# Combination weights in slot order inside the experts' inner product, the layer gate multiplied by POOL ahead of the store, and the final scaling done tile by tile

## The chip, the cores and the metric

The kernel runs on one core of one Trainium2 chip. The metric is the device time of one execution in microseconds (us). In what follows PE is TensorE, DVE is VectorE, ACT is ScalarE, POOL is GpSimd and SP is SyncE, which here only issues DMAs. L1413 means line 1413 of the kernel as the profile counts it.

## The reference, cut to what matters

One layer for 128 context tokens and 512 latent tokens (640 rows, five tiles of 128) of width 1024. The mixer (mLSTM and differential attention) is untouched. What the change touches is the mixture of experts, its gate and the final norm:

```python
h = rmsnorm(x, norm_ffn) * (1.0 + sc2) + sh2
x = x + g2 * hierarchical_moe(h, ...)      # g2 differs between context and latent tokens
y = rmsnorm(x, final_norm)
...
# hierarchical_moe: top-1 of 4 groups, then top-2 of 4 experts in it
comb = jnp.sum(one_hot(expert_idx, 16) * (top_p * p_grp)[..., None], axis=1)
for e in range(16):
    a, u = jnp.split(x @ w_gu[e], 2, axis=-1)
    y = y + comb[:, e:e + 1] * ((silu(a) * u) @ w_dn[e])
```

## The kernel before, in words

Every engine runs a program of its own, written out by hand; the order of the work on an engine is the order of the text, and engines wait for each other on semaphores.

**Output projection and routing.** For each of the five tiles PE computes the projection in two halves (`oproj`, L1599), DVE adds the gated residual (`residual`, L1210 and L1211), ACT makes the norm, DVE writes the modulated rows h2 (`modulate`, L1225 and L1227), SP stores them to a scratch tensor in DRAM, PE transposes them (L1634) and computes 20 router logits (L1645). DVE turns these into one-hot picks (`route`, L1138 to L1162), PE ranks the picks within each expert (L1652), DVE builds a placement matrix (`place_rank`, L1169 to L1171) and PE multiplies it with the token numbers (`slot_ids`, L1662), so that slot s of expert e holds a token number (`place_id`, `idall`). `place_slot` (L1190 to L1201) computes for each token where its two results will lie, and the two weights of its two picks. DVE works through these in the order of the loop `for t in range(NT)`: rank of t-2, residual, id and slot of t-2, route of t-1, second residual, modulate of t. SP's queue in the same stage holds, in this order: the four broadcast loads of scale and shift (`mod2`), the two of the layer gate g2 (`g2b`), the final norm's vector, the weights of the first two experts, the stores of h2.

**The experts.** A round gives each expert 128 slots; the routing decides at run time how many rounds there are (`n_rounds`), and this input takes one. Within a round the 16 experts go through in 8 pairs (b = 0, 1). POOL gathers 128 rows of h2 for each expert of a pair (L602, an indirect DMA) one pair ahead; PE transposes them into the PSUM banks 2b and 2b+1 (L1706); DVE copies them out (L1269); PE multiplies by the gate and up weights (L1713); ACT makes silu (L824); DVE multiplies it with u (L1274); PE transposes that (L1720, L1734); DVE copies (L1277); PE multiplies by the down weights into the same banks 2b and 2b+1 (L1728); ACT copies the result to SBUF (L828, L829) and stores it to a second scratch tensor (L831). The transposes of the next pair wait until ACT has emptied the banks (`yo_ready`). SP streams the weights.

**After the experts.** POOL gathers for each token tile the rows of its two picks (ten indirect DMAs, L612). ACT scales the first by its weight (L840), DVE multiplies the second by its weight and adds (L1308), multiplies by g2 (L1309) and adds to x (L1311); ACT sums the squares and makes the reciprocal root (L843 to L848). After the last round DVE scales each tile by that and by the final norm's vector (L1318), and SP stores it (L484).

Of the kernel before, what the change touches and what calls it, by code (L numbers as in the profile page):

```python
# [17 lines left out]
ALU = mybir.AluOpType  # L18
# [70 lines left out]
def build_body(nc, ctx, a, out, scratch):  # L89
# [114 lines left out]
    pid = TMP[:, 10748:10908].rearrange("p (t j n) -> p t j n", t=NT, j=2)  # L204
    idacc = TMP[:, 10908:10924]
# [17 lines left out]
    consts_ready = sem("consts_ready")  # L223
# [73 lines left out]
    g2_loaded = sem("g2_loaded")  # L297
# [35 lines left out]
    pick_w = sem("pick_w")  # L333
    y_scaled = sem("y_scaled")
# [43 lines left out]
    def _(sp):  # L378
# [76 lines left out]
        for c in range(2):  # L455
            sp.dma_start(g2b[:, c, :], rows[c, 3 * D:4 * D].partition_broadcast(P)).then_inc(g2_loaded, 16)
# [28 lines left out]
        sp.wait_ge(outs, 16 * (NT + 5))  # L485
# [3 lines left out]
    def _(pool):  # L489
# [23 lines left out]
        nc.gpsimd.memset(ones4[:], 1.0).then_inc(consts_ready, 1)  # L513
# [9 lines left out]
        pool.wait_ge(consts_ready, 1)  # L523

# [62 lines left out]
        pool.wait_ge(slots_ready, NT)  # L587
        pool.wait_ge(rounds_ready, 1)
        n_rounds = pool.value_load(rnd[0:1, 0:1], min_val=1, max_val=ROUNDS)
        with pool.Fori(0, n_rounds) as r:  # L590
            pool.wait_ge(idall_ready, r + 1)
            pool.sem_inc(pool_turn, 1)
            with pool.Fori(0, PAIRS) as q:
                it = r * PAIRS + q

                for b in range(2):
                    pool.wait_ge(xg_T[b], it + 1)
                nc.gpsimd.tensor_copy(idp[:], idall[:, bass.ds(q * 2, 2)]).then_inc(idp_ready, 1)  # L598
                pool.wait_ge(idp_ready, it + 1)
                pool.sem_inc(pool_turn, 1)  # L600
                for b in range(2):
                    pool.indirect_dma_start(out=xg[:, b, :], out_offset=None, in_=scratch["h2"],  # L602
                                            in_offset=bass.IndirectOffsetOnAxis(ap=idp[:, b:b + 1], axis=0)
                                            ).then_inc(xg_in[b], 16)
# [3 lines left out]
            pool.wait_ge(y_sum, r * NT + 2)  # L608
# [12 lines left out]
    def _(act):  # L621
# [195 lines left out]
        act.sem_inc(fin_rstd, NT)  # L817
        act.sem_inc(x2_ready, NT)
        with act.Fori(0, n_rounds) as r:
            with act.Fori(0, PAIRS) as q:  # L820
# [4 lines left out]
                for b in range(2):  # L825
# [4 lines left out]
                    act.wait_ge(yo_ready[b], it + 2)  # L830
# [3 lines left out]
            for t in range(NT + 1):  # L834
                if t < NT:
                    act.wait_ge(pick_in[t], r * 32 + 32)
                    if t == 0:
                        act.wait_ge(pick_w, r + 1)
                    y0 = ypick[t][0]
                    nc.scalar.activation(y0, y0, ACT.Copy, scale=rs[:, 20, t:t + 1]).then_inc(y_scaled, 1)  # L840
                if t >= 1:
                    act.wait_ge(y_sum, r * NT + (t + 2))
                    nc.scalar.activation(junkn, x1[:, t - 1, :], ACT.Square, accum_out=stat[:, t - 1:t]).then_inc(x2_ready, 1)  # L843
                    act.wait_ge(x2_ready, r * NT + (NT + t))
                    nc.scalar.activation(stat[:, 7 + t:8 + t], stat[:, t - 1:t], ACT.Ln, scale=1.0 / D,
                                         bias=stat[:, 60:61]).then_inc(fin_ln, 1)
                    act.wait_ge(fin_ln, r * NT + t)
                    nc.scalar.activation(stat[:, 15 + t:16 + t], stat[:, 7 + t:8 + t], ACT.Exp, scale=-0.5).then_inc(fin_rstd, 1)  # L848
# [3 lines left out]
    def _(dve):  # L852
# [361 lines left out]
        def modulate(t):  # L1214
# [3 lines left out]
            if t == 0:  # L1218
                dve.wait_ge(mod_loaded, 64)
# [544 lines left out]
```

## Time and profile before

| | us |
|---|---|
| three runs of the kernel before | 781.37, 781.39, 783.45 (median 781.39) |
| the profiled execution | 778.9 |
| its span, first to last instruction | 777.1 |
| PE busy, share of the span | 674.7, 87% |
| DVE busy | 338.3, 44% |
| ACT busy | 174.3, 22% |
| POOL busy | 101.9, 13% |
| mean granted clock of PE, of full speed | 0.946 |

All positions below are us from the start of this one execution's span. The chain of waits follows the work that ended last backwards, always to what released it; PE's share of that chain is 75%, DVE's 10%. A busy engine off the chain costs nothing in itself. The experts run from about 543 to 738, and what comes behind them from there to 777.1.

### The profile page before, as it was taken

To read this page: it belongs to the slowest core of one execution; us is meant where nothing else is said; L and a number is where in the kernel's file an instruction comes from. 1 tells how busy PE (TensorE), PEld (TensorE's weight loads), DVE (VectorE), ACT (ScalarE), POOL (GpSimd) and SP (SyncE) were. 2 spreads that over 40 slices of the span, in tenths; PEclk is the share of its full clock that TensorE was granted. 3 is DMA by queue.
4 is the path that set the end of the run, shared out by engine and by line. 5 is a ranking of instruction groups with operands and counts; after the bars stand their busy time and mean duration, and the time that the engine had idled before them with its cause. 6 is when DMAs were issued, how large, how long until landed. Compare 5 with 4: busy or idle time off the path is not lost.

```text
span 777.1 us, 7561 instructions
## 1 busy us (share of the span) xinstructions
PE 674.7 (87%) x2657; PEld 363.0 (47%) x2657; DVE 338.3 (44%) x733; ACT 174.3 (22%) x417; POOL 101.9 (13%) x133
## 2 busy tenths in 40 slices
PE   3899999799999999986889999983899999999910
PEld 1444574245556555543567544542444444444410
DVE  2254353321545533568888166674111211112157
ACT  5000200001211111113677322211021201121143
POOL 1231000021101120002532100001111001110050
PEclk9999999999999999998999999995899999999955
DMA  8998414903130210204000395000599999999273
GB/s 292 387 347 295 171 52 148 313 2 135 42 130 17 95 58 13 109 0 163 0 1 1 137 355 213 28 27 32 179 357 345 340 358 362 360 357 342 100 282 151
DMA packets 62962, 137.86 MB, mean 177 GB/s; under 512 B 4614, under 2 KB 11102, under 8 KB 62932
## 3 DMA queue, kind: packets, MB, share of 16 engines
q1 hardware_dynamic: 53000, 112.41, 40.9%
q0 software_dynamic: 5248, 15.63, 5.6%
q10 hardware_dynamic: 4684, 9.44, 3.1%
q8 instruction: 17, 0.28, 0.2%
q14 instruction: 13, 0.11, 0.0%
HBM read 122.69 MB, written 14.74 MB: 177 GB/s over the span
## 4 chain that ended last, share of the span: by engine, by line
PE 75%; DVE 10%; DMA 5%; issue 4%; SPq 3%; ACT 2%; DVEq 0%; POOL 0%; POOLq 0%; ACTq 0%
PE PS L1413 25%; PE PS L1713 14%; PE PS L1728 7%; PE PS L1599 7%; PE PS L1405 4%; DMA PR<-in_w_ada 3%; PE PS L1444 2%; PE PS L1588 1%; DVE PR L953 1%; PE PS L1645 1%; PE PS L1518 1%; PE PS L1706 1%; PE PS L1492 1%; DVE stat L1082 1%; SPq L400 1%
## 5 line engine op out<-in xcount | busy, mean ns | idle before, releaser
L1413 PE MATMUL PS<-RING,hT 128*128 128x512 f32 x480 | 215.6, 598 | 1.3 <-DVE hT L909 1.3
L1413 PEld LDWEIGHTS PS<-RING,hT 128*128 128x128 f32 x480 | 88.4, 191 | 102.6 <-issue 102.1
L1713 PE MATMUL PS<-PR,RING 128*128 128x512 f32 x256 | 113.2, 595 | 0.1
L1713 PEld LDWEIGHTS PS<-PR,RING 128*128 128x128 f32 x256 | 47.4, 190 | 55.3 <-issue 53.6
L1599 PE MATMUL PS<-RING,hT 128*128 128x512 f32 x160 | 72.5, 606 | 0.0
L1728 PE MATMUL PS<-PR,RING 128*128 128x512 f32 x128 | 57.6, 592 | 0.0
L1599 PEld LDWEIGHTS PS<-RING,hT 128*128 128x128 f32 x160 | 30.1, 195 | 33.3 <-issue 33.3
L1269 DVE COPY RING<-PS 128x512 f32<-128x512 f32 x32 | 20.6, 686 | 50.2 <-PE PS L1706 49.6
L1274 DVE TENSOR_TENSOR RING<-RING,PS 128x256 f32<-128x256 f32 x16 | 6.8, 422 | 77.3 <-ACT RING L824 77.3
L1728 PEld LDWEIGHTS PS<-PR,RING 128*128 128x128 f32 x128 | 23.7, 190 | 26.8 <-issue 26.8
L1405 PE MATMUL PS<-hT,RING 128*128 128x512 f32 (+3 forms) x128 | 35.4, 435 | 0.0
L890 DVE TENSOR_TENSOR TMP<-PS,TMP 2x512 f32<-2x512 f32 x24 | 16.4, 682 | 38.2 <-PE PS L1444 37.6
L598 POOL COPY idp<-idall 128x2 uint32 x8 | 1.5, 183 | 233.6 <-PE PS L1706 128.6
L824 ACT ACTIVATE RING<-PS 128x256 f32<-128x256 f32 x16 | 6.1, 383 | 114.2 <-PE PS L1713 114.2
L730 ACT ACTIVATE TMP<-PS,stat 128x640 f32<-128x640 f32 (+1 forms) x40 | 28.2, 706 | 8.1 <-DVE stat L1082 7.7
L1706 PE MATMUL PS<-ident,RING 128*128 128x128 f32 x128 | 18.3, 290 | 13.1 <-DMA RING<-scratch_h,idp 10.2
L545 POOL TENSOR_TENSOR TMP<-TMP 128x512 f32<-128x512 f32 x10 | 13.4, 1337 | 119.7 <-DMA TMP<-scratch_gfr 118.6
L1405 PEld LDWEIGHTS PS<-hT,RING 128*128 128x128 f32 x128 | 21.6, 190 | 12.6 <-issue 7.6
L1082 DVE TENSOR_REDUCE stat<-PS 128x2 f32<-128x1280 f32 (+1 forms) x20 | 25.5, 1273 | 4.6 <-PE PS L1556 4.4
L1706 PEld LDWEIGHTS PS<-ident,RING 128*128 128x128 f32 x128 | 15.5, 150 | 18.7 <-issue 18.3
L1573 PE MATMUL PS<-ident,TMP 128*128 128x128 f32 x68 | 12.1, 295 | 12.2 <-DVE TMP L1101 6.9
L935 DVE COPY PR<-PS 128x512 f32<-128x512 f32 x15 | 10.3, 689 | 25.7 <-PE PS L1435 25.6
(304 smaller groups left out, 899.6 us busy)
## 6 DMA issues: line engine op xcount, KB each, us to landing
PR<-in_w_gate_up SPq DMA_DIRECT2D x16, 2048.0 KB, 10.4
PR<-in_w_ada SPq DMA_DIRECT2D x20, 1024.0 KB, 13.3
PR<-in_w_down SPq DMA_DIRECT2D x16, 1024.0 KB, 13.4
RING<-in_w_in SPq DMA_DIRECT2D x14, 1024.0 KB, 7.5
scratch_y<-RING ACTq DMA_DIRECT2D x16, 512.0 KB, 7.2
RING<-in_w_ada SPq DMA_DIRECT2D x4, 1024.0 KB, 13.6
RING<-in_w_out SPq DMA_DIRECT2D x4, 1024.0 KB, 6.2
TMP<-scratch_gfr SPq DMA_DIRECT2D x10, 256.0 KB, 4.9
```

What stands on the lines that cost most here:

```text
L545: nc.gpsimd.tensor_tensor(mbuf[:, g % 2], mbuf[:, g % 2], masks[:, d, :].unsqueeze(1).broadcast_to([P, H, P]), ALU.add).then_inc(mb_ready, 1)
L730: nc.scalar.activation(pexp[:, u % 3, m, 0:nk], scores[u % 2][:, m, 0:nk], ACT.Exp, bias=stat[:, 40 + 2 * (u % 3) + m:41 + 2 * (u % 3) + m ...
L890: step(V.tensor_tensor(row, PS[32 * g:32 * g + 2, 4, :], row, ALU.add))
L1082: V.tensor_reduce(stat[:, 40 + 2 * (u % 3):42 + 2 * (u % 3)], scores[u % 2][:, :, 0:nk], AX.X, ALU.max, negate=True).then_inc(smax, 1)
L1269: last = V.tensor_copy(xgT[:, b, 4 * k2:4 * k2 + 4, :], PS[:, 2 * b + k2, :].rearrange("p (k s) -> p k s", k=4))
L1405: last = mm(PS[:, m % 2, o:o + hi - lo], ring[:, ci % 2, k, h * P:(h + 1) * P], hTv[:, k, lo:hi], start=(k == 0), stop=(k == KD - 1))
L1413: last = mm(PS[:, m % 2, :], hTv[:, k, t * P:(t + 1) * P], ring[:, ci % 2, k, :], start=(k == 0), stop=(k == KD - 1))
L1444: last = mm(PS[g:g + 2, 4, :], silc[:, k, :], ada_w2[n_ % 2][:, k, :], start=(k < 4), stop=(k >= 4), tile_position=(0, g))
L1599: last = mm(PS[:, i % 4, :], hTv[:, k, t * P:(t + 1) * P], ring[:, (WOUT + q) % 2, k, :], start=(k == 0), stop=(k == KD - 1))
L1706: last = tr(PS[:, 2 * b + k // 4, (k % 4) * P:(k % 4 + 1) * P], xg[:, b, k * P:(k + 1) * P], ident[:])
L1713: last = mm(PS[:, 4 + b, :], xgT[:, b, k, :], gub[b][:, k, :], start=(k == 0), stop=(k == KD - 1))
L1728: last = mm(PS[:, 2 * b + q, :], hidT[:, b, k, :], dnb[b][:, k, q * 512:(q + 1) * 512], start=(k == 0), stop=(k == 1))
```

## The change

Three things are done at another place.

1. The combination weight of a slot is found in slot order. `route` now computes the two weights of each token (four more operations, behind the one-hot picks) and puts the picks times the weights beside the picks times the token number, so `slot_ids` multiplies 32 columns instead of 16; the result is `wm`. In the loop the weight multiplies silu(a) * u as DVE's per-partition operand, in the instruction that was there already.
2. The layer gate g2 multiplies the expert's result ahead of its store: DVE builds a gate row per slot (`gate2`, context or latent), two operations of 1024 columns per pair, and POOL multiplies `yo` by it. ACT, which copies and stores, now waits for POOL between its copy and its store. DVE's operations with weights and g2 behind the gathers, and ACT's scaling there, go away.
3. The final scaling of tile t-1 follows the sum of tile t inside the loop over tiles, into the buffer of the gathered rows; ACT issues the stores of the output instead of SP. Slots of other rounds are read from a row of zeros that POOL writes to the scratch tensor beforehand.

Beside this `modulate(0)` waits for all six broadcast loads (`mod_loaded` at 96), not for four; POOL waits for the slots of the tokens only behind the experts, not ahead of them; `place_slot` has as many operations as before; and DVE subtracts the two rows of g2 once ahead of the loop.

The diff, cut to its core:

```diff
@@ SP
-            sp.dma_start(g2b[:, c, :], rows[c, 3 * D:4 * D].partition_broadcast(P)).then_inc(g2_loaded, 16)
+            sp.dma_start(g2b[:, c, :], rows[c, 3 * D:4 * D].partition_broadcast(P)).then_inc(mod_loaded, 16)
...
-        for t in range(NT):
-            sp.wait_ge(fin_ready, t + 1)
-            dst = out["y_prompt"][0] if t == 0 else out["y_sample"][0, (t - 1) * P:t * P, :]
-            sp.dma_start(dst, x1[:, t, :]).then_inc(outs, 16)
@@ POOL
-        pool.wait_ge(slots_ready, NT)
+        step(nc.gpsimd.memset(zrow, 0.0))
+        pool.dma_start(scratch["y"][ZROW:ZROW + 1, :], zrow).then_inc(row_stored, 16)
+        pool.wait_ge(row_stored, 16 * 9)
         pool.wait_ge(rounds_ready, 1)
...
+        def gate_y(it):
+
+            for b in range(2):
+                pool.wait_ge(g2_ready[b], it + 2)
+                pool.wait_ge(yo_ready[b], it + 2)
+                pool.sem_inc(pool_turn, 1)
+                nc.gpsimd.tensor_tensor(yo[:, b, :], yo[:, b, :], gate2[:, b, :], ALU.mult).then_inc(y_gated[b], 1)
...
+            gather(r * PAIRS, idall[:, 0:2])
+            with pool.Fori(1, PAIRS) as q:
                 it = r * PAIRS + q
...
+                gather(it, idall[:, bass.ds(q * 2, 2)])
+                gate_y(it - 1)
+            gate_y(r * PAIRS + (PAIRS - 1))
@@ ACT
                     nc.scalar.activation(yo[:, b, 512:D], PS[:, 2 * b + 1, :], ACT.Copy).then_inc(yo_ready[b], 1)
-                    act.wait_ge(yo_ready[b], it + 2)
+                    act.wait_ge(y_gated[b], it + 2)
                     act.dma_start(scratch["y"][bass.ds(q * 256 + b * P, P), :], yo[:, b, :]).then_inc(yo_stored[b], 16)
...
-                    act.wait_ge(pick_in[t], r * 32 + 32)
-                    if t == 0:
-                        act.wait_ge(pick_w, r + 1)
-                    y0 = ypick[t][0]
-                    nc.scalar.activation(y0, y0, ACT.Copy, scale=rs[:, 20, t:t + 1]).then_inc(y_scaled, 1)
+                    act.wait_ge(y_sum, r * NT + (t + 1))
+                    nc.scalar.activation(junkn, x1[:, t, :], ACT.Square, accum_out=stat[:, t:t + 1]).then_inc(x2_ready, 1)
...
                 if t >= 1:
+                    act.wait_ge(fin_ready, r * NT + t)
+                    dst = out["y_prompt"][0] if t == 1 else out["y_sample"][0, (t - 2) * P:(t - 1) * P, :]
+                    act.dma_start(dst, ypick[t - 1][0]).then_inc(outs, 16)
@@ DVE, route(t)
-            V.tensor_scalar(pid[:, t], r16[:, 0:2, t, :], misc[:, 32 + t:33 + t], None, ALU.mult)
+            V.tensor_scalar(pid[:, t, :, 0:NE], r16[:, 0:2, t, :], misc[:, 32 + t:33 + t], None, ALU.mult)
+            dve.wait_ge(route_exp, t + 1)
+            step(V.scalar_tensor_tensor(R(8), R(2), 1.0, R(7), ALU.add, ALU.mult))
+            step(V.reciprocal(R(9), R(8)))
+            V.tensor_scalar(pid[:, t, 0, NE:2 * NE], r16[:, 0, t], R(9), None, ALU.mult)
+            V.tensor_scalar(pid[:, t, 1, NE:2 * NE], r16[:, 1, t], R(9), R(2), ALU.mult, ALU.mult)
@@ DVE, place_id(NT - 1)
-                V.tensor_tensor(idall[:], PS[:, 6, 32:48], idacc, ALU.add).then_inc(idall_ready, 1)
+                step(V.tensor_tensor(idall[:], PS[:, 6, 32:48], idacc[:, 0:NE], ALU.add))
+                dve.sem_inc(idall_ready, 1)
+                V.tensor_tensor(wm[:, :, 0], PS[:, 6, 48:64], idacc[:, NE:2 * NE], ALU.add)
+                V.tensor_scalar(wm[:, :, 1], idall[:], float(CTX), None, ALU.is_lt)
@@ DVE, modulate(t)
             if t == 0:
-                dve.wait_ge(mod_loaded, 64)
+                dve.wait_ge(mod_loaded, 96)
@@ DVE, the pairs
-                    V.tensor_tensor(hid[:, b], sil[:, b], PS[:, 4 + b, EH:2 * EH], ALU.mult).then_inc(hid_ready[b], 1)
+                    V.scalar_tensor_tensor(hid[:, b], sil[:, b], wmc[:, b, 0:1], PS[:, 4 + b, EH:2 * EH], ALU.mult, ALU.mult
+                                           ).then_inc(hid_ready[b], 1)
...
+                for b in range(2):
+                    dve.wait_ge(y_gated[b], it + 1)
+                    V.scalar_tensor_tensor(gate2[:, b], g2b[:, 0], wmc[:, b, 1:2], g2b[:, 1], ALU.mult, ALU.add
+                                           ).then_inc(g2_ready[b], 1)
@@ DVE, behind the gathers
-                rstep(V.scalar_tensor_tensor(y0, y1, rs[:, 21, t:t + 1], y0, ALU.mult, ALU.add))
-                rstep(V.tensor_tensor(y0, y0, g2b[:, c], ALU.mult))
...
+                    rstep(V.tensor_tensor(y0, y0, y1, ALU.add))
+                    V.tensor_tensor(x1[:, t], x1[:, t], y0, ALU.add).then_inc(y_sum, 1)
+                if t >= 1:
+                    dve.wait_ge(fin_rstd, r * NT + t)
+                    V.scalar_tensor_tensor(ypick[t - 1][0], x1[:, t - 1], stat[:, 15 + t:16 + t], fnorm[:], ALU.mult, ALU.mult
+                                           ).then_inc(fin_ready, 1)
```

## Rows read from the trace of the kernel before

**Rows 1.** Windows, one pair: length, busy (count) per engine, PE clock, DMA.

```profile
571.95:595.60 23.65, 23.25 (x68) 11.17 (x68) 4.27 (x8) 4.22 (x8) 2.10 (x3) 1.00 0.97 347
```

**Rows 2.** Chain of waits between two pairs: start, length, what.

```profile
571.08 0.60 ACT RING L828
...
572.31 1.06 PE PS L1706 x8
573.38 10.57 PE PS L1713 x24
```

**Rows 3.** Timeline of DVE and ACT (ACTq: its DMA issue) ahead of that.

```profile
565.93 0.42 DVE L1277 COPY RING<-PS 128x256 f32<-128x256 f32 x1 [1.10 <-PE PS L1734]
567.74 0.60 ACT L828 ACTIVATE RING<-PS 128x512 f32<-128x512 f32 x1 [3.36 <-PE PS L1728]
568.23 0.59 ACT L829 ACTIVATE RING<-PS 128x512 f32<-128x512 f32 x1
569.01 0.36 ACTq L831 DMA_DIRECT2D scratch_y<-RING  x1
```

**Rows 4.** POOL's products by line: shortest, median, longest ns.

```profile
L560 POOL TENSOR_TENSOR TMP<-TMP x20: 389/398/975, 390.3 to 432.0; 128x128 f32<-128x128 f32 x20
L568 POOL TENSOR_TENSOR PR<-HM x5: 1040/1042/1042, 353.6 to 357.5; 128x512 f32<-128x512 f32 x5
L576 POOL TENSOR_TENSOR HM<-HM,PR x5: 1267/1270/1723, 378.7 to 388.6; 128x512 f32<-128x512 f32 x5
```

**Rows 5.** Timeline, where DVE and POOL both read pairs of SBUF operands.

```profile
383.33 1.98 DVE L1101 SCALAR_TENSOR_TENSOR TMP<-TMP,stat 128x640 f32<-128x640 f32 x1
...
384.58 1.63 POOL L575 TENSOR_TENSOR HM<-HM,stat 128x512 f32<-128x512 f32 x1
```

**Rows 6.** Instructions on scratch_mod, the second load of g2b.

```profile
L456 SPq DMA_DIRECT2D PR<-scratch_mod x1: 892/892/892, 448.8 to 448.8; - x1
DMA to landing us min/median/max: 9.1/9.1/9.1
```

**Rows 7.** Timeline of the routing stage: DVE, PE's weight load, POOL.

```profile
455.89 0.75 DVE L1225 SCALAR_TENSOR_TENSOR HM<-TMP,stat 128x512 f32<-128x512 f32 x1 [1.35 <-ACT stat L810]
...
475.12 0.15 DVE L1193 SCALAR_TENSOR_TENSOR TMP<-TMP 128x1 f32<-128x1 f32 x1
...
475.50 0.16 DVE L1195 TENSOR_TENSOR TMP<-TMP 128x1 f32<-128x1 f32 x1
...
492.02 0.52 PEld L1662 LDWEIGHTS PS<-TMP 128*128 128x128 f32 x4 [0.68 <-DVE TMP L1171]
...
534.08 0.19 DVE L1169 TENSOR_TENSOR TMP<-PS,TMP 128x32 f32<-128x32 f32 x1 [0.38 <-PE PS L1656]
...
536.69 0.15 DVE L1250 TENSOR_SCALAR rnd<-cnt 128x1 int32<-128x1 f32 x1
...
538.77 0.16 DVE L1201 SCALAR_TENSOR_TENSOR slot<-TMP 128x2 uint32<-128x2 f32 x1
...
540.70 0.18 POOL L598 COPY idp<-idall 128x2 uint32 x1 [104.92 <-issue]
```

**Rows 8.** Chain of waits behind the last pair.

```profile
737.89 2.62 DMA scratch_y<-RING
```

**Rows 9.** Timeline behind the gathers: ACT and DVE.

```profile
747.38 1.15 ACT L840 ACTIVATE hT<-hT,TMP 128x1024 f32<-128x1024 f32 x1 [7.71 <-DMA hT<-scratch_y,slot]
...
751.14 1.22 DVE L1311 TENSOR_TENSOR TMP<-TMP,hT 128x1024 f32<-128x1024 f32 x1
...
767.25 1.06 ACT L843 ACTIVATE PR<-TMP 128x1024 f32<-128x1024 f32 x1 [2.00 <-DVE TMP L1311]
767.53 6.07 DVE L1318 SCALAR_TENSOR_TENSOR TMP<-TMP,stat,fnorm 128x1024 f32<-128x1024 f32 x5 [0.31 <-DVE TMP L1311]
...
768.76 0.20 ACT L848 ACTIVATE stat<-stat 128x1 f32<-128x1 f32 x1
```

**Rows 10.** Windows, columns as in rows 1.

```profile
759.00:762.00 3.00, 0.00 (x0) 0.00 (x0) 2.97 (x3) 2.11 (x5) 0.00 (x0) 0.50 0.00 1
```

More of the change, by code:

```diff
@@ L332, in build_body @@
     pick_in = [sem(f"pick_in{t}") for t in range(NT)]
-    pick_w = sem("pick_w")
-    y_scaled = sem("y_scaled")
+    g2_ready = [sem(f"g2_ready{b}") for b in range(2)]
+    y_gated = [sem(f"y_gated{b}") for b in range(2)]
     y_sum = sem("y_sum")
@@ L512, in _ @@
         pool.dma_start(bgate[:], a["b_gate"][0].unsqueeze(1)).then_inc(early_loaded, 16)
-        nc.gpsimd.memset(ones4[:], 1.0).then_inc(consts_ready, 1)
+        step(nc.gpsimd.memset(ones4[:], 1.0))
         def load_bias2(n_):
@@ L592, in _ @@
             pool.sem_inc(pool_turn, 1)
-            with pool.Fori(0, PAIRS) as q:
+            gather(r * PAIRS, idall[:, 0:2])
+            with pool.Fori(1, PAIRS) as q:
                 it = r * PAIRS + q
[L596 to L604, printed above, removed]
+                gather(it, idall[:, bass.ds(q * 2, 2)])
+                gate_y(it - 1)
+            gate_y(r * PAIRS + (PAIRS - 1))
             for b in range(2):
                 pool.wait_ge(yo_stored[b], r * (PAIRS * 16) + (PAIRS * 16 + 16))
-            pool.wait_ge(y_sum, r * NT + 2)
+            pool.wait_ge(slots_ready, r + NT)
+            pool.wait_ge(outs, r * (16 * NT) + 16 * 5)
             pool.sem_inc(pool_turn, 1)
@@ L1190, in place_slot @@
             step(V.tensor_tensor(prod, expert, picks, ALU.mult))
[L1191 to L1195 removed]
+            step(V.tensor_reduce(rs[:, 14:16, t], prod, AX.X, ALU.add))
             r2, e2, b2, s2 = (rs[:, i:i + 2, t] for i in (12, 14, 16, 18))
@@ L1258, in _ @@
             dve.sem_inc(hidT_ready[b], 1)
-        dve.sem_inc(y_sum, 2)
+        dve.wait_ge(fnorm_loaded, 16)
+        step(V.tensor_tensor(g2b[:, 0], g2b[:, 0], g2b[:, 1], ALU.subtract))
+        for b in range(2):
+            dve.sem_inc(g2_ready[b], 1)
         base = n[0]
-        PER_ROUND = 3 + 3 * NT
+        PER_ROUND = 4 + 2 * NT
         with dve.Fori(0, n_rounds) as r:
@@ L1264, in _ @@
                 it = r * PAIRS + q
+                for b in range(2):
+                    dve.wait_ge(g2_ready[b], it + 1)
+                V.tensor_copy(wmc, wm[:, bass.ds(q * 2, 2), :])
                 for b in range(2):
@@ L1278, in _ @@
                                   ).then_inc(hidT_ready[b], 1)
+                for b in range(2):
+                    dve.wait_ge(y_gated[b], it + 1)
+                    V.scalar_tensor_tensor(gate2[:, b], g2b[:, 0], wmc[:, b, 1:2], g2b[:, 1], ALU.mult, ALU.add
+                                           ).then_inc(g2_ready[b], 1)
             n[0] = 0
@@ L1322, in _ @@
+            rstep(V.scalar_tensor_tensor(rs[:, 20:22], rs[:, 16:18], 0.0, rs[:, 18:20], ALU.is_equal, ALU.mult))
+            rstep(V.tensor_scalar(slot[:, 2:4], rs[:, 20:22], float(ZROW), None, ALU.add))
+            dve.sem_inc(slots_ready, 1)
+            assert n[0] == PER_ROUND
     @block.tensor
@@ L1661, in slot_ids @@
             for j in range(2):
-                last = mm(PS[:, 6, 32:48], rmat[:, t % 2, j, :], pid[:, t, j, :], start=(j == 0), stop=(j == 1))
+                last = mm(PS[:, 6, 32:64], rmat[:, t % 2, j, :], pid[:, t, j, :], start=(j == 0), stop=(j == 1))
             last.then_inc(ids_done, 1)
```

85 lines of the change are left out of this document (42 added, 43 removed).

## The prediction

> **What bounds the kernel now.** I read the chain of waits first, to see where the end is set, then windows and timelines of three stretches that the edits touch. Inside the experts PE sets the pace: of a pair's 23.65 us PE is busy 23.25, at a granted clock of 1.00, which is the 2.4 GHz level, while DVE has 4.27, ACT 4.22 and POOL 2.10 [rows 1]. The DMA engines are at 0.97 there, but the chain doesn't pass through them. The one wait in that chain is between pairs: ACT's two copies of expert b=1 begin at 571.08, and only then can PE transpose the next pair's b=1 rows, at 572.31, and go on at 573.38 [rows 2]. So whatever makes ACT later at 571.08 makes every pair longer. In the routing stage the chain runs through DVE, and behind the gathers it is DVE alone. The reader is to see that the change takes work from the last stretch and puts waits into the first two.
>
> **Inside the pairs.** DVE's weight rides in an instruction that was there already: nothing. DVE's two gate rows per pair come behind the copy at 565.93, which lasts 0.42 [rows 3]; at 1.2 us each (five of this form took 6.07 [rows 9]) plus the last one's drain they are done at about 568.9,. They are covered, with 2 us to spare: what DVE does next waits for PE's transposes at the pair's end [rows 2]. If that cover were gone each would cost its 1.2 us.
>
> POOL's product is the heavy part. ACT copies expert b=0 from 567.74 to 568.82 and issued its store at 569.01 for 0.36 [rows 3]. Now it waits for POOL in between, and what is queued behind that wait on ACT is its copy of b=1, for which PE waits. A POOL product of 1024 columns isn't in the trace. With two different operands 512 columns take 1268 ns; one operand read twice takes 398 for 128 columns and 1042 for 512, a slope of 1.68 ns a column [rows 4]. A start cost of 398 - 128 x 1.68 = 184 ns leaves 1084 for 512 columns, so 2.35 us for 1024. Low bound: 1268 + 512 x 1.68 = 2.13; high bound twice 1268, 2.54. I take 2.35. Start at 568.95 (0.13 for the hop from ACT), end at 571.30, store issued 0.19 later as in the row, 0.36 of issuing, 0.12 to the copy: 571.97 against 571.08, late by 0.89. Everything behind it moves: seven boundaries cost 6.2 us. If issuing the store doesn't hold ACT's next copy, it is 0.53 each.
>
> The Trainium skill (GPSIMD Engine Reference, Elementwise — side-by-side cycle accounting) gives some 2.6 cycles an element for a product of two tensors and 4497 ns for 2048 columns; half of that, 2.25, is an estimate from the page, and by it the seven boundaries would cost 5.5 and the last pair 0.2 less.
>
> The product of b=1 starts when PE goes on, and what waits for it is that expert's store and, behind it on POOL, a gather one pair ahead; it moves by some 2.5 us and its rows are needed a pair, 23.65 us, later [rows 1]: nothing. ACT's silu waits behind it too, but for a PE product that has just begun: nothing either. At the last pair there is no next pair to hide it: the copy 0.89 late, then product and hop 2.5, in front of the 2.62 us store that the chain passes [rows 8]. Together 3.4.
>
> **Routing.** `modulate(0)` started at 455.89 [rows 7]. The second load of g2b is issued at 448.85 and lands 9.1 later, at 457.95 [rows 6]: 2.1 late, and DVE, then PE's transposes and the logits are late by it. Its bounds are 0, if the end of the tile's chain had slack, and 2.1. Four more operations per `route`: two dependent ones at 0.19 each, as from 475.12 to 475.50 [rows 7], and two independent ones, for which I take 0.15 each: 0.69. Is this on the path? For tile 0 and tile 3 DVE's chain is the path: 0.69 each. For tiles 1 and 2 PE's weight load at 492.02 sat idle for 0.68 and was released by DVE too [rows 7], though PE itself shows no idle time there; I take the slack as under 0.1, so 0.62 each. For tile 4 DVE sat idle 0.38 before 534.08 waiting for PE [rows 7], and 0.69 leaves about 0.2. Sum 2.8. If all tiles had slack, this is 0.7. In `place_id(4)` one completion wait and two small operations stand ahead of the number of rounds: 0.35.
>
> Against it, POOL no longer waits for the slots: the number of rounds was written by 536.84, the last slot by 538.93, and the index copy came at 540.70 [rows 7]. That gives back 2.1. POOL's memset and store of the zero row lie between the last store of h2 and the number of rounds, under the wait for the latter, while DVE routes the last tile. The queue of SP is issued in the same order, so no weight load moves. Routing in all: 2.1 + 2.8 + 0.35 - 2.1 = 3.2 later.
>
> **Behind the gathers.** Count from the landing of the first two rows, at 747.34 [rows 9]; the end is 777.1, so 29.8. DMA is idle from 759 [rows 10], so the last rows come 12 us after the first, at most 3.1 per tile; that stays. New DVE work: two additions at 1.25 (1.22 and its gap [rows 9]) and a final scaling at 1.28 per tile. Tile 0 is summed at 2.5; tile 1 landed at 3.1, is summed at 5.6, and tile 0 scaled at 6.9. From here DVE is the bound: each tile 3.8, so tile 4 is summed at 17.0 and tile 3 scaled at 18.3. ACT's chain from 767.25 to 768.96 is 1.7 [rows 9], so the last reciprocal root is there at 18.8 and the last scaling ends at 20.1. The last scaling before ended at 773.6 [rows 9] and the span at 777.1, so the last store and the close take 3.5: 23.6. That saves 6.2. Bounds: 8.8 if only the last tile's chain were left behind the last landing (12 + 2.5 + 1.7 + 1.3 + 3.5 = 21.0), and 3 if the stores, now beside the gathers, hold the rows back.
>
> **Sum.** 3.2 + 6.2 + 3.4 - 6.2 = +6.6. It is made against the profiled execution, 778.9, of which 777.1 is span: 785.5. The median of the three runs, 781.39, is 2.5 above that execution, so on the median it is 788.0.
>
> **The rivals.**
> First, DVE and POOL get in each other's way. Where both ran on pairs of SBUF operands, DVE's operation took 1.98 and POOL's 1.63 [rows 5], against 1.04 for 512 columns of one tensor [rows 4]. DVE's second gate row ends at 568.9 and POOL starts at 568.95, so it is a matter of 0.05. If they meet, each boundary and the last pair lose about 0.6 more: +4.8, 792.8. Against it: DVE's other work in the window reads PSUM. The Trainium skill (SBUF — State Buffer, Who interferes with whom) says that a DVE instruction with two SBUF inputs and a POOL instruction that reads SBUF exclude each other, the second waiting for the first's end; by that rule a gate row that is late by x costs x, up to its 1.2 a pair. The overlap seen in rows 5 agrees in kind.
>
> Second, smaller waits: issuing the store doesn't hold ACT (8 x 0.36 = 2.9 less) and the wait for g2b is mostly slack (up to 2.1 less): 783.0 with both, 785.1 with the first alone.
>
> Third, on the other side, the loop doesn't get longer. Expert b=1 is ready 3.34 after b=0; the copies take 1.08 and hops and issue 0.8, so a product of up to 1.46 us is hidden. Then 3.2 + 1.6 - 6.2 = -1.4: 780.0, no measurable change. For it speaks only that POOL's spans are rough; against it every POOL row, since 1.46 would be 1.25 ns a column where even one operand costs 1.68.
>
> Fourth, the last stretch doesn't give what the change says: stores and gathers share the DMA engines, 3 instead of 6.2: 791.2.
>
> **How the numbers follow.** Forecast 0.60 (its own range 786 to 790.5), first rival 0.12, second 0.15, third 0.06, fourth 0.07. A measurement of this kernel tells about 0.3%, 2.3 us, from no change. The third rival and the lowest corner of the second are within it, 0.08; faster needs the third rival together with a g2b that is there in time, 0.03, taken from these two; slower 0.89. The range 784.0 to 792.0 leaves out the third rival, the first one's upper part and the second's lowest part.
>
> **What would show it.** In the changed profile: ACT's copy of b=1 starts about 0.9 later behind b=0 than 3.34, PE idle between pairs is about 1.3 instead of 0.4, and a pair takes 24.5. POOL's product reads 2.1 to 2.5 us. `modulate(0)` is released by a DMA at about 458. The first index copy comes at about 544, and from the first landed rows to the end it is 24 us. The prediction is wrong if POOL's product is under 1.5 or over 3 us, if the pair stays at 23.65, or if the first gather doesn't move.

## The result, and the profile after

The changed kernel took 790.04 us (median of 5 runs, 786.2 to 791.44); the kernel before, run beside it on the same chip, 781.39 (5 runs, 778.33 to 783.45). The ratio is 1.0102, with a 95% interval of 1.0076 to 1.0128: slower by 8.65 us, where the prediction had +6.6 and 788.0.

The profiled execution of the changed kernel took 791.44, of which 789.6 is span; that of before 778.9, of which 777.1 is span. The two spans differ by 12.5. That is 3.9 more than the medians do, since one execution lies 1.4 above its median and the other 2.5 below. The table cuts the two spans at the same events. Each time is read from the timelines, in us from its own span's start.

| event | before | after | stretch grew by | forecast |
|---|---|---|---|---|
| PE starts the mixer's last transposes, ahead of every edited line | 443.68 | 446.22 | 2.54 | 0 |
| first index copy of the pairs (L598) | 540.70 | 550.18 | 6.94 | 3.2 |
| ACT's copy of b=0 in the first pair | 567.74 | 578.89 | 1.67 | 0 |
| the same in the eighth pair: seven boundaries | 733.29 | 748.80 | 4.36 | 6.2 |
| last store of y issued | 737.89 | 756.93 | 3.53 | 3.4 |
| first rows of the gathers landed | 747.34 | 767.02 | 0.64 | 0 |
| end | 777.1 | 789.6 | -7.2 | -6.2 |

The first row is nothing that the change did: the same event lies between 444.98 and 447.79 in the executions of the experiments too. Without it the stretches sum to 9.9, against +8.65 between the medians.

The timeline of the changed kernel at the end of `modulate(0)`'s wait, and tile 0's and tile 1's work behind it, answers to the first lines of [rows 7]. In brackets is the idle time before, and what ended it.

```profile
460.80 0.75 DVE L1247 SCALAR_TENSOR_TENSOR HM<-TMP,stat 128x512 f32<-128x512 f32 x1 [3.71 <-DMA PR<-scratch_mod]
...
462.42 0.63 PE L1663 MATMUL PS<-ident,HM 128*128 128x128 f32 x4 [3.36 <-DVE HM L1249]
...
480.25 1.06 PE L1691 MATMUL PS<-HM,TMP 128*128 128x32 f32 x4 [2.31 <-DVE TMP L1191]
481.12 1.95 PE L1663 MATMUL PS<-ident,HM 128*128 128x128 f32 x8
482.86 5.66 PE L1628 MATMUL PS<-RING,hT 128*128 128x512 f32 x8
```

The wait is there: DVE was idle 3.71 and a landing of `scratch_mod` ended it, where it was idle 1.35 and released by ACT in [rows 7]. Further down, PE's items are slow. The eight L1628 at 482.86 took 5.66, the same eight of before 5.07 at 474.87:

```profile
473.28 0.62 PE L1662 MATMUL PS<-TMP 128*128 128x16 f32 x4 [1.60 <-DVE TMP L1171]
...
474.87 5.07 PE L1599 MATMUL PS<-RING,hT 128*128 128x512 f32 x8
```

Windows of the same stretch, in the changed kernel (stretch, length, then busy time and count of PE, its weight loads, DVE, ACT and POOL, then granted clock, DMA share, GB/s):

```profile
464.00:470.00 6.00, 6.00 (x27) 4.00 (x27) 1.59 (x7) 1.50 (x4) 0.00 (x0) 0.79 1.04 396
476.00:482.00 6.00, 3.69 (x13) 2.32 (x12) 5.10 (x12) 0.48 (x2) 0.00 (x0) 0.85 0.58 230
482.00:488.00 6.00, 6.00 (x14) 3.00 (x13) 1.59 (x10) 2.10 (x5) 0.00 (x0) 0.58 0.00 0
```

And in the kernel before:

```profile
464.00:470.00 6.00, 6.00 (x16) 2.68 (x15) 4.27 (x22) 1.61 (x7) 0.00 (x0) 1.00 1.03 392
470.00:476.00 6.00, 4.39 (x18) 2.59 (x17) 5.50 (x18) 1.48 (x3) 0.00 (x0) 0.87 1.04 408
476.00:482.00 6.00, 6.00 (x25) 3.48 (x25) 0.81 (x5) 0.61 (x3) 0.00 (x0) 0.85 0.10 40
```

In both kernels the clock leaves its upper level (1.00, 2.4 GHz) behind an idle time of PE. In the changed one it does so right behind the 3.36 us in which PE waited for `modulate(0)`, and once more behind tile 0's 2.31 (1.60 in before), where it comes down to 0.58, near the lower level of 1.2 GHz.

The boundary between two pairs, in the timeline of the changed kernel, answers to [rows 2, 3] and to this line of before:

```profile
572.31 1.06 PE L1706 MATMUL PS<-ident,RING 128*128 128x128 f32 x8 [0.39 <-ACT RING L829]
```

In the changed kernel:

```profile
577.42 2.47 DVE L1309 SCALAR_TENSOR_TENSOR PR<-PR,HM 128x1024 f32<-128x1024 f32 x2
...
578.89 0.60 ACT L845 ACTIVATE RING<-PS 128x512 f32<-128x512 f32 x1 [3.36 <-PE PS L1757]
...
580.15 2.37 POOL L612 TENSOR_TENSOR RING<-RING,PR 128x1024 f32<-128x1024 f32 x1 [16.61 <-ACT RING L846]
...
582.71 0.36 ACTq L848 DMA_DIRECT2D scratch_y<-RING  x1
...
583.18 0.60 ACT L845 ACTIVATE RING<-PS 128x512 f32<-128x512 f32 x1 [3.21 <-POOL RING L612]
...
584.41 1.06 PE L1735 MATMUL PS<-ident,RING 128*128 128x128 f32 x8 [1.34 <-ACT RING L846]
...
585.31 10.46 PE L1742 MATMUL PS<-PR,RING 128*128 128x512 f32 x24
```

Read it as a relay. ACT's copies end, POOL multiplies for 2.37, ACT issues the store for 0.36, and only then comes the copy of b=1, 4.29 behind that of b=0 instead of 3.34. PE waits for it 1.34 instead of 0.39. This is the first boundary; at the next six the copy comes 4.23 or 4.24 behind. One pair of 24.26, in the windows, against 23.65 in [rows 1]:

```profile
578.89:603.15 24.26, 22.92 (x69) 11.14 (x68) 6.88 (x12) 4.22 (x7) 6.82 (x5) 1.00 0.95 344
```

Behind the last pair the chain of waits now has POOL's product ahead of the store of [rows 8]:

```profile
754.44 2.33 POOL RING L612
...
756.93 2.62 DMA scratch_y<-RING
```

Behind the gathers, the timeline of the changed kernel answers to [rows 9]:

```profile
767.02 1.23 DVE L1339 TENSOR_TENSOR hT<-hT 128x1024 f32<-128x1024 f32 x1 [6.36 <-DMA hT<-scratch_y,slot]
768.28 1.22 DVE L1340 TENSOR_TENSOR TMP<-TMP,hT 128x1024 f32<-128x1024 f32 x1
...
770.34 1.23 DVE L1339 TENSOR_TENSOR hT<-hT 128x1024 f32<-128x1024 f32 x1 [0.84 <-DMA hT<-scratch_y,slot]
...
776.34 1.28 DVE L1343 SCALAR_TENSOR_TENSOR hT<-TMP,stat,fnorm 128x1024 f32<-128x1024 f32 x1
...
779.92 1.28 DVE L1343 SCALAR_TENSOR_TENSOR hT<-TMP,stat,fnorm 128x1024 f32<-128x1024 f32 x1
...
783.51 1.28 DVE L1343 SCALAR_TENSOR_TENSOR TMP<-TMP,stat,fnorm 128x1024 f32<-128x1024 f32 x1
...
785.37 1.28 DVE L1343 SCALAR_TENSOR_TENSOR TMP<-TMP,stat,fnorm 128x1024 f32<-128x1024 f32 x1 [0.58 <-ACT stat L859]
```

DVE goes from tile to tile in 3.59 with no idle time, which is two additions and a scaling, and the end comes 22.6 behind the first landing instead of 29.8.

### The profile page after: what moved, and what is told of

Same layout as the page of the kernel before. It is cut to its first block and busy times, and to the rows that moved or that the text cites. A ratio compares the mean times of both kernels' runs of the same rounds, so it can differ in the third digit from the quotient of the medians.

```text
span 789.6 us, 7639 instructions
## 1 busy us (share of the span) xinstructions
PE 681.9 (86%) x2657; PEld 368.2 (47%) x2657; DVE 359.4 (46%) x778; ACT 168.7 (21%) x412; POOL 141.9 (18%) x151
## 5 line engine op out<-in xcount | busy, mean ns | idle before, releaser
L1628 PE MATMUL PS<-RING,hT 128*128 128x512 f32 x160 | 74.1, 616 | 0.0
L612 POOL TENSOR_TENSOR RING<-RING,PR 128x1024 f32<-128x1024 f32 x16 | 37.9, 2371 | 136.2 <-ACT RING L846 121.3
L1628 PEld LDWEIGHTS PS<-RING,hT 128*128 128x128 f32 x160 | 30.7, 199 | 34.3 <-issue 34.3
L1301 DVE SCALAR_TENSOR_TENSOR RING<-RING,HM,PS 128x256 f32<-128x256 f32 x16 | 7.7, 481 | 76.5 <-ACT RING L841 76.5
L1434 PE MATMUL PS<-hT,RING 128*128 128x512 f32 (+3 forms) x128 | 37.1, 450 | 0.0
L1735 PEld LDWEIGHTS PS<-ident,RING 128*128 128x128 f32 x128 | 15.7, 151 | 23.5 <-issue 22.6
## 6 DMA issues: line engine op xcount, KB each, us to landing
RING<-in_w_ada SPq DMA_DIRECT2D x4, 1024.0 KB, 12.5
```

Source lines behind the costliest of these rows:

```text
L612: nc.gpsimd.tensor_tensor(yo[:, b, :], yo[:, b, :], gate2[:, b, :], ALU.mult).then_inc(y_gated[b], 1)
L1434: last = mm(PS[:, m % 2, o:o + hi - lo], ring[:, ci % 2, k, h * P:(h + 1) * P], hTv[:, k, lo:hi], start=(k == 0), stop=(k == KD - 1))
L1628: last = mm(PS[:, i % 4, :], hTv[:, k, t * P:(t + 1) * P], ring[:, (WOUT + q) % 2, k, :], start=(k == 0), stop=(k == KD - 1))
L1735: last = tr(PS[:, 2 * b + k // 4, (k % 4) * P:(k % 4 + 1) * P], xg[:, b, k * P:(k + 1) * P], ident[:])
```

## The experiments

"Before" in each comparison is the kernel before on the same chip: 781.85 beside e1, e2, e3 and e5 (20 runs), 782.23 beside e4, e6, e7 and e8 (17 runs). Against its 781.39 the changed kernel stood at 1.0102.

**e1: g2b isn't awaited in the routing stage.** Its loads get a semaphore of their own again, which DVE awaits ahead of the pairs.

```diff
-            sp.dma_start(g2b[:, c, :], rows[c, 3 * D:4 * D].partition_broadcast(P)).then_inc(mod_loaded, 16)
+            sp.dma_start(g2b[:, c, :], rows[c, 3 * D:4 * D].partition_broadcast(P)).then_inc(g2_loaded, 16)
...
-                dve.wait_ge(mod_loaded, 96)
+                dve.wait_ge(mod_loaded, 64)
...
         dve.wait_ge(fnorm_loaded, 16)
+        dve.wait_ge(g2_loaded, 32)
         step(V.tensor_tensor(g2b[:, 0], g2b[:, 0], g2b[:, 1], ALU.subtract))
```

> The changed kernel, but modulate(0) waits for the four loads it reads, as before the change; the two loads of g2b are awaited ahead of the pairs. Theory: that wait costs 2.4 us at modulate(0), and the longer idle time of PE behind it lowers the granted clock, which costs some 2 us more in the next 30 us; so modulate(0) is again released by ACT's reciprocal root, the clock in the stretch up to the second tile's logits is back at the level before, and the time is 785.5 to 787.5 instead of 790.0. Rival (the clock has nothing to do with it): 787.6 and the low clock stays. Second rival (slack behind it, the wait is free): 789.5 to 790.5, with another wait in its place.

Measured: 787.26, ratio 1.0058 (1.0039 to 1.0077). That is inside the expected range, but only 0.3 from the rival's 787.6, so the time does not choose between them and the trace has to. Between the two profiled executions the stretch from the mixer's transposes to the index copy is 98.6 instead of 104.0: 5.4 less for 2.4 of direct delay. Timeline, then windows, of e1:

```profile
458.51 0.75 DVE L1248 SCALAR_TENSOR_TENSOR HM<-TMP,stat 128x512 f32<-128x512 f32 x1 [1.35 <-ACT stat L830]
...
460.13 0.63 PE L1665 MATMUL PS<-ident,HM 128*128 128x128 f32 x4 [1.00 <-DVE HM L1250]
```

```profile
464.00:470.00 6.00, 6.00 (x25) 3.52 (x25) 3.83 (x28) 0.39 (x3) 0.00 (x0) 1.00 1.03 395
476.00:482.00 6.00, 5.40 (x18) 3.63 (x19) 3.69 (x16) 2.10 (x5) 0.00 (x0) 0.72 0.54 221
482.00:488.00 6.00, 6.00 (x27) 3.61 (x26) 2.55 (x19) 0.00 (x0) 0.00 (x0) 1.00 0.00 0
```

PE is idle 1.00 instead of 3.36, and the clock is 1.00 in 464 to 470 (0.79 with the wait) and in 482 to 488 (0.58). From the transposes to tile 1's logits it takes 38.7, against 44.0 with the wait and 38.0 in the kernel before. The rival, by which the low clock stays, is out.

The 5.4 is one pair of executions, and the whole kernel gains less: 0.44 points of the ratio, 3.4 us. The kernels of e2, e5, e7 and e8 below have the routing code of the changed kernel, the wait included, so their traces tell how far the cost varies. Behind tile 1's logits all five take the same 58.2 to the number of rounds; they differ ahead of it.

| execution | wait for g2b | PE idle behind it | transposes to tile 0's logits (clock) | from there to tile 1's (clock) |
|---|---|---|---|---|
| before | no | 1.00 | 19.24 (1.00) | 18.75 (0.91) |
| e1 | no | 1.00 | 19.24 (1.00) | 19.45 (0.91) |
| e8 | yes | 3.32 | 22.58 (0.92) | 17.77 (1.00) |
| e7 | yes | 3.20 | 22.95 (0.93) | 19.44 (0.91) |
| e5 | yes | 3.18 | 23.04 (0.93) | 19.44 (0.91) |
| e2 | yes | 3.04 | 22.47 (0.92) | 20.98 (0.84) |
| changed kernel | yes | 3.36 | 22.97 (0.93) | 21.07 (0.84) |

The last column's windows for e8 and the changed kernel, with the clock third from the end:

```profile
468.41:486.18 17.77, 15.46 (x58) 8.32 (x58) 12.03 (x52) 3.60 (x12) 0.00 (x0) 1.00 0.60 229
469.19:490.26 21.07, 18.76 (x58) 10.29 (x58) 12.03 (x52) 3.71 (x12) 0.00 (x0) 0.84 0.50 193
```

So the wait's cost has two parts. Up to tile 0's logits it is 3.2 to 3.8 in all five, more than the 2.4 of delay, at a mean clock of 0.92 or 0.93 instead of 1.00. Between the two logits, behind the idle time of 2.31 that all of them have, the clock is lower than in e1 in two executions (1.5 and 1.6 more), the same in two, and higher in one (1.7 less). In all the wait costs 1.7 to 5.3 against e1, 3.9 in the mean, near the 3.4 of the medians. Why the second part comes out so differently is open.

In e1's profiled execution the first pair took 30.03 from index copy to ACT's copy of b=0 instead of 28.71, and there too the granted clock stayed low for longer.

**e2: ACT copies both experts first, then stores.** The product stays as it is.

```diff
                     nc.scalar.activation(yo[:, b, 512:D], PS[:, 2 * b + 1, :], ACT.Copy).then_inc(yo_ready[b], 1)
+                for b in range(2):
                     act.wait_ge(y_gated[b], it + 2)
                     act.dma_start(scratch["y"][bass.ds(q * 256 + b * P, P), :], yo[:, b, :]).then_inc(yo_stored[b], 16)
```

> The changed kernel, but ACT makes the copies of both experts of a pair before it waits for POOL's products and issues the two stores. Theory (ACT's copy of expert 1 is held behind POOL's product of expert 0): the pair goes from 24.31 back to 23.65 us and the last pair's copy comes 0.95 earlier: 5.6 less, 784.4. Rival (the product makes the pair longer in another way: it collides with DVE's gate rows, or puts off the gathers): the pair stays at 24.2 or more and the time at 789 to 790.5.

Measured: 782.67, ratio 1.0010 (0.9996 to 1.0023). Timeline of e2 at the boundary:

```profile
580.51 2.37 POOL L612 TENSOR_TENSOR RING<-RING,PR 128x1024 f32<-128x1024 f32 x1 [16.68 <-ACT RING L846]
...
582.59 0.60 ACT L845 ACTIVATE RING<-PS 128x512 f32<-128x512 f32 x1 [2.26 <-PE PS L1758]
...
583.07 0.36 ACTq L849 DMA_DIRECT2D scratch_y<-RING  x1
...
583.82 1.06 PE L1736 MATMUL PS<-ident,RING 128*128 128x128 f32 x8 [0.39 <-ACT RING L846]
```

POOL's product takes the same 2.37, yet ACT's copy is released by PE and PE waits 0.39 as in the kernel before. The pair is 23.56. So it was not the product that made the pairs longer, but that the copy of b=1 stood behind the wait for it. From the copy of b=0 in the last pair to the last store it takes 7.10 instead of 8.13. The seven boundaries and the last pair give 6.0 in the traces, where 5.6 was expected; by the ratios it is 0.92 points, 7.2 us, and the time is 1.7 below the expected 784.4.

**e5: half the product.** POOL multiplies columns 0 to 511 of each row alone. The other half of the experts' rows is stored without its gate.

```diff
-                nc.gpsimd.tensor_tensor(yo[:, b, :], yo[:, b, :], gate2[:, b, :], ALU.mult)
+                nc.gpsimd.tensor_tensor(yo[:, b, 0:512], yo[:, b, 0:512], gate2[:, b, 0:512], ALU.mult)
```

> The changed kernel, but POOL multiplies only columns 0 to 511 of each result by the layer gate; columns 512 to 1023 stay without the gate. Theory (the hold is the product's length less the 1.46 us between the two experts' results that nothing else fills): the product takes 1.27 us, under that, so the pair is at 23.65, as with the copies first; the last pair has 0.95 and 1.1 less: 783.4. Rival (a fixed cost of the hop to POOL and back, not its length): the pair stays above 24.1.

Measured: 781.64, ratio 0.9999 (0.9977 to 1.0022). Timeline of e5:

```profile
580.55 1.28 POOL L612 TENSOR_TENSOR RING<-RING,PR 128x512 f32<-128x512 f32 x1 [17.50 <-ACT RING L846]
...
582.63 0.60 ACT L845 ACTIVATE RING<-PS 128x512 f32<-128x512 f32 x1 [2.26 <-PE PS L1757]
```

The product is 1.28, the wait is gone though ACT's order is that of the changed kernel, and the pair is 23.56 again. A product of 1.28 is hidden, which is in line with the 1.46 up to which the prediction's third rival had it hidden; at 1024 columns it just isn't that short. The time is again 1.8 below the expected one, 783.4.

**e3: the weights' operations in DVE's slack.** The wait for `route_exp` and the four instructions of `route` that make the weights move to a function of their own, called behind the next tile's `residual(t, 1)`.

```diff
             V.tensor_scalar(pid[:, t, :, 0:NE], r16[:, 0:2, t, :], misc[:, 32 + t:33 + t], None, ALU.mult)
+        def route_weights(t):
             dve.wait_ge(route_exp, t + 1)
...
             residual(t, 1)
+            if t >= 1:
+                route_weights(t - 1)
...
         route(NT - 1)
+        route_weights(NT - 1)
```

> The changed kernel, but the four operations that make the two weights come behind the tile's second residual, where DVE waits for ACT's reciprocal root anyway. Theory: they cost about 0.65 us for each of tiles 0 to 3 where they stood, on DVE's chain, and nothing here: 2.5 less, 787.5, more if PE's shorter idle times keep its clock up. Rival (the chain has slack there and only the wait for g2b counts): 789.5 to 790.5.

Measured: 785.98, ratio 1.0046 (1.0028 to 1.0064). The tiles' logits follow each other in 17.05 as in the kernel before; in the changed one in 17.77. From transposes to index copy it is 99.9 instead of 104.0. Half of these 4.1 lie between the logits of tile 1 and the last tile's (48.4 instead of 50.5; 48.1 in before). The other half lies ahead of tile 1's logits, 42.0 from the transposes instead of 44.0; there only tile 0's four operations, some 0.7, were moved away. Against e5 and e7, which have the operations in their old place and the same clock between the logits (0.91), it is only 0.4 shorter, so the rest of this half goes with the clock. The time is 1.5 below the expected 787.5.

**e4: e1, e2 and e3 together.** It asks whether the three costs are separate.

> The changed kernel with the three edits together: no wait for g2b at modulate(0), both copies ahead of POOL's products, the weights' four operations in the gap ahead of modulate. Theory (the loss is these three waits, and the gain behind the gathers is real): the stretch from the mixer's last transposes to the first index copy is 95.5 us (97.0 in the kernel before, 104.0 in the changed one), the pair 23.57, behind the first landed rows 22.6 as in the changed kernel against 29.8 before; the last pair keeps 2.4 for POOL's product. In all 776, that is 0.7% under the kernel before. Rival (there is another cost, of the clock or of POOL, that the three edits don't take away): 780 or more.

Measured: 777.02, ratio 0.9930 (0.9909 to 0.9951). This is faster than both kernels, by 0.7% than the one before. Routing takes 95.8 (97.0 in before), a pair 23.56, and from the first landing to the end 23.0. The savings of e1, e2 and e3, by their ratios 0.44, 0.92 and 0.56 points, add up to 1.92; e4 has 1.72. The expected 776 and the expected stretches of 95.5, 23.57 and 22.6 are near; the clock up to tile 0's logits is 1.00 again, and 0.91 from there to tile 1's, as in the kernel before.

**e6: no gate in the pairs.** POOL's product, the gate rows and `gate_y` go; ACT stores as in the kernel before, and DVE multiplies each tile's sum by g2b behind the gathers. The edits of e1 and e3 are in it.

```diff
-                    act.wait_ge(y_gated[b], it + 2)
+                    act.wait_ge(yo_ready[b], it + 2)
...
                     rstep(V.tensor_tensor(y0, y0, y1, ALU.add))
+                    rstep(V.tensor_tensor(y0, y0, g2b[:, min(t, 1)], ALU.mult))
```

> The changed kernel without POOL's product: the layer gate is multiplied by DVE behind the gathers again, 5 operations of 1.24 us, while the weights stay in slot order in the experts' inner product and the final scaling stays tile by tile; no wait for g2b at modulate(0), weights' operations in the gap. Theory: the pair is 23.65; the store of the last pair is 2.5 earlier than with POOL's product, but DVE is the bound behind the gathers with 5.05 per tile, 28.5 from the first landed rows to the end against 22.6: 779.5, above the version with POOL's product and the three edits by some 3.5. Rival (the gathers bound that stretch, so DVE's extra operations are hidden): 775.

Measured: 778.95, ratio 0.9954 (0.9937 to 0.9971). The last stretch is 28.0, so five products of 1.22 there cost 5.0 against e4's 23.0. Since the pairs need no gate, 4.6 lie between the copy of b=0 in the last pair and the last store, against e4's 7.1. The ratios differ by 0.24 points, 1.9 us, in favour of the gate in the pairs, where 3.5 was expected. The two intervals overlap, so this difference is only just told.

**e7: the slots' wait put back.** `pool.wait_ge(slots_ready, NT)` stands ahead of the wait for `rounds_ready` again.

> The changed kernel, but POOL waits for all slots ahead of the first gather, as before the change. Theory: the first index copy comes 2.1 later behind the number of rounds (3.9 to 4.0 instead of 1.8): 792. Rival (the first pair is held by something else, its weights or the clock): 790.

Measured: 792.23, ratio 1.0134 (1.0099 to 1.0168). From the number of rounds to the index copy it is 3.97; with the change 1.76, so the wait taken away gave 2.2 (forecast 2.1). The interval of its ratio overlaps that of the changed kernel, so this rests on the trace, not on the time. The trace shows something more. Timelines of e7, DVE and POOL:

```profile
549.31 1.23 DVE L1282 TENSOR_TENSOR PR<-PR 128x1024 f32<-128x1024 f32 x1 [1.39 <-issue]
549.51 1.07 POOL L599 COPY idp<-idall 128x2 uint32<-128x2 uint32 x1 [11.59 <-issue]
...
552.80 0.96 POOL L603 DMA_INDIRECT RING<-scratch_h,idp  x1 [0.30 <-issue]
```

In the changed kernel the index copy comes before DVE's subtraction of the two gates, and the second gather meets it:

```profile
550.18 0.18 POOL L598 COPY idp<-idall 128x2 uint32<-128x2 uint32 x1 [9.38 <-PEq L1727]
...
552.20 1.23 DVE L1281 TENSOR_TENSOR PR<-PR 128x1024 f32<-128x1024 f32 x1 [1.39 <-issue]
552.59 1.67 POOL L602 DMA_INDIRECT RING<-scratch_h,idp  x1 [0.30 <-issue]
```

Whichever POOL instruction starts inside the subtraction is the long one: 1.07 instead of 0.18 for the copy (it ends at 550.58, the subtraction at 550.54), 1.67 instead of 0.96 for the gather (it ends at 554.26, the subtraction at 553.43). In all seven profiled executions in which the second gather met the subtraction it took 1.67 to 1.75, in the three others 0.96.

**e8: all sums, then all scalings.** Behind the gathers DVE adds five tiles and then scales five; what is computed per tile is as in the changed kernel.

```diff
-            for t in range(NT + 1):
+            for t in range(2 * NT):
                 if t < NT:
                     dve.wait_ge(pick_in[t], r * 32 + 32)
...
-                if t >= 1:
-                    dve.wait_ge(fin_rstd, r * NT + t)
+                else:
+                    u = t - NT
+                    dve.wait_ge(fin_rstd, r * NT + u + 1)
```

> The changed kernel, but the five final scalings and their stores come behind all five sums. Theory: of the 7.2 us that the changed kernel saves behind the first landed rows, most comes from the operations that are gone, since DVE then waits for landing rows; the order gives the rest: here the last scaling ends 1.3 later and five stores come close together, 0.6 more: 24.5 from the first landed rows to the end, 792. Rival (the order tile by tile is what gives the gain): 27 or more, 795.

Measured: 789.58, ratio 1.0099 (1.0071 to 1.0127): not to be told from the changed kernel. Timeline of e8:

```profile
776.49 3.67 DVE L1345 SCALAR_TENSOR_TENSOR hT<-TMP,stat,fnorm 128x1024 f32<-128x1024 f32 x3
780.07 2.47 DVE L1345 SCALAR_TENSOR_TENSOR TMP<-TMP,stat,fnorm 128x1024 f32<-128x1024 f32 x2
```

Its last stretch is 23.3 against 22.6, where I had expected 24.5. The last scaling ends 19.5 behind the first landing, as early as in the changed kernel (19.6); what is longer is the end behind it, 3.7 instead of 3.0, where five stores come close together. In these two traces the order "tile by tile" is worth 0.7 of the 7.2 (the other executions with that order and the same work there have 22.0 to 23.0); the rest comes from the operations that are gone. DVE has the same 18 us of work in either order (five times 3.59), and little of it has to wait for a landing.

## Why the prediction was right, and where it was off

The direction and the places held, and so did the range: 790.04 lies in 784.0 to 792.0. The forecast's 788.0 is 2 us short. That it is so near is partly luck, because the terms' errors partly cancel: between the two traces routing cost 3.7 more than forecast and the first pair 1.7, while the boundaries cost 1.8 less and the last stretch gave 1.0 more. The first two vary by some us from execution to execution.

**The routing term was mis-sized: 3.2 forecast, 6.9 in this execution, 5.4 in the mean of the five with the same routing code (3.3 to 6.9, with e7's slots' wait taken out).** Cut at the logits, the changed kernel's trace against that of before reads so. From the mixer's transposes to tile 1's logits 6.0 were lost (44.0 against 38.0), where the prediction has 2.1 for g2b and 0.69 for tile 0's weights. From there to the number of rounds it is 3.1 (58.2 against 55.0), where it has 2.5. From there to the index copy 2.25 were gained, where it has 2.1, and e7 confirms that term. So nearly the whole error, 3.2 of 3.7, lies in the first part. There g2b's landing released `modulate(0)`, as forecast, and held DVE 2.4 longer (3.71 against 1.35). What the sum lacked is what can follow from a longer idle PE: the stretches that lose more than the wait's length are those with a granted clock of 0.79 and 0.58. The step that failed is "2.1 late, and DVE, then PE's transposes and the logits are late by it", with 0 and 2.1 as bounds: the cost of a wait was bounded by its own length. In its place the runs show 3.2 to 3.8 by tile 0's logits in all five executions, and 3.4 for the whole kernel by the medians. By tile 1's logits it is 1.7 to 5.3; e8's 1.7 is within the bound only because the clock stayed up behind the next idle time. That the clock is the carrier rests on this: the same code is the longer the lower its clock (17.77 at 1.00, 19.44 at 0.91, 20.98 and 21.07 at 0.84), and PE's items are longer there. No run set the clock by itself. Rows that could have warned were there in the trace of before: 0.87 and 0.85 in 470 to 482, around an idle time of PE of 1.60 that ended at 473.28. The Trainium skill (TensorE: Matmul & The Clock Gate, HAM oscillation — how this bites in real kernels) tells of a matmul kernel in which PE's wait for a DMA brings the clock down so that the work behind the wait starts at the lower level. The traces agree in kind: the mean clock up to tile 0's logits is 0.92 or 0.93 in all six executions with the wait, e3's among them, and 1.00 in the four without it.

**The hold between pairs was right in mechanism: 0.89 forecast, 0.62 measured.** ACT's copy of b=1 is 0.95 late at the first boundary and 0.89 or 0.90 at the others, and the product took 2.37 for 2.35, so every link of that chain was sized well. The last link was not: that the pair grows by as much as the copy is late. Between the start of PE's second group of transposes and its next product it took 1.07 before and takes 0.90 now (585.31 - 584.41), since DVE's copy of b=0's rows, which that product needs, is done by 584.40. The 24 products behind it take 10.46 instead of 10.57. Both together give back 0.28 of the 0.90. In e2 the first of these times is 0.99 and a pair 23.56; DVE's copy starts 1.07 behind the first transposes there and 1.16 in the kernel before. Why it does is open. The forecast signs, 0.9 later, PE idle 1.3 and a pair of 24.5, read 0.95, 1.34 and 24.26.

**The last pair** was right: 3.4 forecast, 3.53 measured.

**The first pair** was not in the sum and cost 1.67. The prediction costed DVE's two gate rows per pair but left out the single subtraction ahead of the pairs, which was an instruction of the change too. It runs into the second gather and makes it 0.7 longer, and PE then waits 0.52 for that expert's rows: from PE's first transposes to its first product it is 4.25 instead of 3.53 (3.64 in e6, which has no subtraction). The rest is in the 24 products that follow, before and in the changed kernel:

```profile
549.81 10.49 PE L1713 MATMUL PS<-PR,RING 128*128 128x512 f32 x24
...
559.88 11.57 PE L1742 MATMUL PS<-PR,RING 128*128 128x512 f32 x24
```

The granted clock over them is 1.00 before and 0.90 in the changed kernel. So some 0.7 of the 1.67 is the subtraction and 1.1 the clock, less 0.1 between the index copy and the transposes. The clock's part varies from execution to execution: in e1 the 24 took 12.51 and the stretch 30.03, in e3 10.47 and 27.44.

**Behind the gathers:** 7.2 saved, 6.2 forecast. DVE's 3.59 a tile was forecast as 3.8, as the instructions overlap a little at their ends; with it the last scaling ends 19.6 behind the first landing, forecast 20.1. The other half is the last store and the close, 3.0 for 3.5. "The stores hold the gathers back" (the fourth rival) is wrong: DVE had no idle time from the second tile's landing until it waited 0.58 for the last tile's root. e8 adds that most of it comes from the removed operations, not from the order.

**The other rivals.** DVE and POOL don't meet between pairs: the gate rows end at 579.89 and POOL starts at 580.15, and all sixteen products took 2371 ns in the mean. The Trainium skill (SBUF — State Buffer, Who interferes with whom) says that a DVE instruction with two SBUF inputs and a POOL instruction that reads SBUF exclude each other. That rule named the right hazard for the wrong place: it agrees with e7's copy, which ends 0.04 behind the subtraction, and not with a loss at the boundaries, where the two are 0.26 apart. The second rival is out for its first part, since ACT's copy did start behind the store's issue, and its second part is the reverse of what happened: the wait for g2b had little slack in any execution (1.7 was the least it cost, in e8). The third is out by the product's 2.37, and e5's 1.28, hidden, is in line with its threshold.

**What stays open:** why the stretch before all edits is 2.5 longer in the profiled execution of the changed kernel (it drifts by some 4 us over all executions), the 0.64 between the last store and the first landing, of which 0.56 lie behind the start of the first gather's issue, and why the clock behind the same idle times falls further in one execution than in another.

## What to carry to other kernels

Ask of a new wait not only how long it is, but who stands behind it in program order: moving ACT's copy of b=1 ahead of the wait for POOL (e2) took away 0.9% with the same work done, and a wait of 2.4 us for a load whose data are needed 90 us later (e1) cost 3.4 by the medians and up to 5.3 in one execution. The work taken off the end stretch, where DVE is nearly without idle time, was a gain there in every execution (22.0 to 28.0 instead of 29.8), and it was worth having once the waits it brought were moved: the same change with three orders mended is 0.7% faster than before instead of 1.0% slower. When an idle time is added to PE in a chain of dependent tiles, look at the granted clock in the windows around the idle times that are there already; if it falls behind them, the added wait's own length is no upper bound. And one pair of traces doesn't size such a cost: the same code lost between 1.7 and 5.3 here, so look at several executions, or at the medians.

## What the runs showed of the hardware

- A PE idle time of 3.36 us instead of 1.00 was followed by granted clocks of 0.79 in 464 to 470 and 0.58 in 482 to 488 instead of 1.00 and 1.00 (the changed kernel against e1), and 2.4 us of direct delay came to 5.3. Over six executions with the wait the mean clock up to tile 0's logits was 0.92 or 0.93, over four without it 1.00. Behind the next idle time of 2.31 the same code took 17.77 at 1.00 (e8), 19.44 at 0.91 (e5, e7) and 21.07 at 0.84 (changed kernel).
- A small POOL copy of 128x2 took 1.07 instead of 0.18 us when it started inside a DVE subtraction of two SBUF tensors, and the issue of an indirect DMA on POOL 1.67 instead of 0.96. The copy ended 0.04 behind the subtraction, the gather's issue 0.83 behind it.
- POOL's product of 1024 columns took 2.37 us, of 512 columns 1.28. The prediction's estimate from shorter ones (2.35) was good to 1%.
- Issuing a store holds what stands behind it in ACT's program: the copy behind it came 0.47 after the issue began (582.71 to 583.18). In e2, where the issue stands behind the copies, it began at 583.07 while they ran (582.59 to 583.67).
